# Norms in pairs, dense matmuls while x arrives, and the second weight block ahead of the taps and gate columns

## Chip, cores and metric

The kernel runs on one core of a Trainium2 chip. The metric is the device time of one execution in microseconds (us), the median over several runs. TensorE is called PE, VectorE DVE, ScalarE ACT, GpSimd POOL and SyncE SP.

## What is computed

One inference step of a two-layer decoder for 256 prompt tokens and 8 sample tokens (264 columns in all). The change touches only the first token mixer, a gated DeltaNet with 8 heads of 128:

```python
def gdn_mixer(x, S0, conv_buf, w_in, conv_w, a_log, dt_bias, norm_w, w_out, chunked):
    proj = x @ w_in                                   # 3072 q,k,v channels, 1024 z, 8 a, 8 b
    qkv = proj[..., :GDN_CONV_CH]
    ...
    qkv_c, new_buf = causal_dwconv(qkv, conv_buf, conv_w)   # 4 taps
    qkv_c = jax.nn.silu(qkv_c.astype(f32))
    ...
    q = l2_normalize(q) * (GDN_DK ** -0.5)
    k = l2_normalize(k)
    g = -jnp.exp(a_log.astype(f32)) * jax.nn.softplus(a.astype(f32) + dt_bias.astype(f32))
    beta = jax.nn.sigmoid(b.astype(f32))
    # chunked delta rule: products of k with k and of q with k, decay masks, a triangular inverse ...
    o = o * lax.rsqrt(jnp.mean(jnp.square(o), axis=-1, keepdims=True) + NORM_EPS) * norm_w.astype(f32)
    o = o * jax.nn.silu(z.astype(f32)).reshape(bsz, t, GDN_HEADS, GDN_DV)
    y = o.reshape(bsz, t, GDN_V_W).astype(x.dtype) @ w_out
```

After it come LayerNorm, a dense SwiGLU, a short convolution mixer and a top-2-of-8 expert SwiGLU. They take most of the time and are not changed.

## The kernel before

Every engine runs a program written out by hand, and semaphores alone join them; within an engine, order is program order. So a wait holds everything that stands behind it on that engine.

All weights pass through one ring of **slots** of 1 MB. SP loads slot n into `raw[n % 7]` (`load`). ACT copies it to `high` as fp32r (`split_high`, a 128x2048 activation), DVE forms the rest in `low` (`split_low`, a 128x2048 tensor_tensor), and PE does 32 matmuls with `high` against the two halves of x (`xh`, `xl`), then 16 with `low` (`dense_slot`, lines L392 and L398; L405, L406 and L414 where other matmuls are woven in). `high` has 3 places (`SPLIT`). `split_high` of slot n+3 stands on ACT behind the copies of slot n's result, and `split_low` of slot n+3 stands on DVE behind the convolution of slot n.

**The first mixer** has 16 slots. Slots 0 to 11 give the 24 q, k and v tiles, two per slot. Their results lie in two alternating pairs of PSUM banks, so PE starts slot n only when DVE has convolved slot n-2 (`conv_done`). Slots 12 to 15 give the z tiles, with the sample tokens' decode matmuls (`decode`) woven in. In each round n of the loop ACT does: scaled copies of slot n's result (L722), `split_high` of n+3, Silu of the tiles of slot n-1 (L731). DVE does: the convolution of slot n (six instructions at L1135 and two copies to `utail`), `split_low` of n+3, then whatever belongs to the round.

**Norms.** The q and k tiles form four groups of four tiles (`g` 0 to 3). A group needs Square on ACT (L751), a matmul with ones on PE (`square_sums`), Ln and Exp on ACT (L762, L769), and a multiplication on DVE (`normalise`). `squares` holds one group. PE's sums stand behind slots 3, 5, 7 and 9; ACT's Ln and Exp are in rounds 3, 5, 7 and 9, each behind a load of the activation table that holds both, and the next Silu loads its own table again. `products(k, f)` on PE (8 matmul calls of 128x128 for each k) form k with k and q with k. `decay_exponent`, `decay_masks`, `key_products` and `query_products` are DVE's part of it; then `TT` is made, eight instructions at L1189 and L1192.

**The end of the projections.** Behind slot 15 PE transposes `TT` (L1800). It waits there for `tt0_ready` and for all four increments of `qkm_ready`, which DVE gives in `query_products`:

```python
            for i in range(4):
                c, g = i // 2, i % 2
                pe.wait_ge(tt0_ready, i + 1)
                pe.wait_ge(qkm_ready, 4)
```

POOL makes one multiplication of this stage, `qkv * gB` (L587, 128x1024), once the second q-with-k products are there (`qkp_psum` 2).

**The start.** PE transposes x (8 rounds of k, each of two 128x128 blocks at L1700 and the 8 sample rows at L1701). ACT and DVE make `xh`, `xl` and the residual copy `xres`. SP's queue: x, the sample rows, slot 0, the convolution taps (four transfers), the 16 gate columns `wab`, then slot 1 and on. PE transposes the taps and forms the gate columns behind slot 0.

Of the kernel before, what the change touches and what calls it, by code (L numbers as in the profile page):

```python
# [7 lines left out]
D = 1024  # L8
KT = D // 128
# [53 lines left out]
def hybrid_step(nc, x_prompt, x_sample, state_gdn_S, state_gdn_conv, state_sconv, ln_g, ln_b, gdn_w_in,  # L63
# [8 lines left out]
    with ExitStack() as ctx:  # L72
# [80 lines left out]
        xsnat = place("xsnat", [8, D], at=tt_at)  # L153
# [7 lines left out]
        squares = place("squares", [128, 4, NP], at=t_at + 12 * D)  # L161
# [278 lines left out]

        def turned(s):

            return 4 * s + (0, 0, 4, 8, 8, 8)[s] if s else 0
# [251 lines left out]
        def _(act):  # L695
# [12 lines left out]
            for n in range(1, SPLIT):  # L708
                split_high(act, n)
            act.wait_ge(nat_T, 2)  # L710
            for i in range(2):
                act.activation(taps[:, 12 * i:12 * i + 12, :],
                               bank[4 + i][:, 0:336].rearrange("p (t c) -> p t c", c=28), ACT.Copy).then_inc(taps_ready, 1)
            act.wait_ge(taps_ready, 2)

            for n in range(OUT0):
# [40 lines left out]
                if n in (3, 5, 7, 9):  # L757
                    g = (n - 3) // 2
                    act.preload_act_table_set("natural_log_exp_and_others")
                    for i in range(2):  # L760
                        act.wait_ge(sq_psum, 2 * g + i + 1)
                        act.activation(squares[:, 2 * i:2 * i + 2, :], bank[4 + 2 * (g % 2) + i][:, :]  # L762
                                       .rearrange("p (t i) -> p t i", t=2), ACT.Ln, bias=eps[:, 0:1]).then_inc(sq_log, 1)
# [4 lines left out]
                    act.wait_ge(sq_log, 2 * g + 2)  # L768
                    act.activation(squares[:, :, :], squares[:, :, :], ACT.Exp, scale=-0.5).then_inc(sq_inv, 1)  # L769
                    if n == 5:  # L770
                        act.wait_ge(gcol_ready, 1)
                        act.activation(nbe[:, :, :], gcol[:, :, 0, :], ACT.Exp).then_inc(nbe_ready, 1)
                    if n == 7:
                        for c in range(NCH):
                            act.wait_ge(d_ready, c + 1)
                            act.activation(DM[:, c, :, :], DM[:, c, :, :], ACT.Exp).then_inc(e_ready, 1)
                    if n == 9:
                        act.wait_ge(sq_log, 9)
                        act.activation(ssq[:, :, :], ssq[:, :, :], ACT.Exp, scale=-0.5).then_inc(sq_inv, 1)
                        act.wait_ge(d_ready, 3)  # L780
                        step(act.activation(kd[:, :, :], kd[:, :, :], ACT.Exp))
                        step(act.activation(egl[:, :], gB[:, :, NP - 1], ACT.Exp))
                        step.wait()
                        act.activation(gB[:, :, :], gB[:, :, :], ACT.Exp).then_inc(eg_ready, 1)
                if n == 12:
                    act.wait_ge(gate_in, 64)
                    act.activation(aS[:, :, :], aS[:, :, :], ACT.Exp).then_inc(aS_ready, 1)
                if n == QT // 2:
                    act.wait_ge(sconv_done, 2)
                    act.activation(qkv[:, 16:24, NP:N], qkv[:, 16:24, NP:N], ACT.Silu).then_inc(ssilu_done, 1)  # L790

# [242 lines left out]
        def _(dve):  # L1034
            step = Steps(dve, dve_step)
            for k in range(KT):
                dve.wait_ge(xh_ready, k + 1)
                step(dve.tensor_copy(xres[:, k, :], bank[k][:, 0:N]))
                dve.tensor_tensor(xl[:, k, :], bank[k][:, 0:N], xh[:, k, :].bitcast(F32), ALU.subtract).then_inc(xl_ready, 1)
            for n in range(SPLIT):  # L1040
                split_low(dve, n)
                if n == 0:
# [18 lines left out]
            def normalise(g):  # L1061
# [3 lines left out]
                if g < 2:  # L1065
                    dve.scalar_tensor_tensor(v, v, 128 ** -0.5, squares[:, :, :], ALU.mult, ALU.mult).then_inc(qk_ready, 1)
                else:
                    dve.tensor_tensor(v, v, squares[:, :, :], ALU.mult).then_inc(qk_ready, 1)
# [50 lines left out]
            for n in range(OUT0):  # L1119
# [3 lines left out]
                if n in (4, 6, 8, 10):  # L1123
                    normalise(n // 2 - 2)
# [38 lines left out]
                if n == 8:  # L1163
                    decay_masks(0)
                if n == 9:
                    decay_masks(1)
                if n == 10:
# [6 lines left out]
                    dve.tensor_tensor(kq[:, :, :], q, k, ALU.mult).then_inc(kq_ready, 1)  # L1174
                if n == 11:
                    sample_conv(16, 24)
                    key_products(0)
                if n == 12:
                    dve.wait_ge(mask_ready, 1 + LEVELS)
                    for c in range(NCH):  # L1180
                        step(dve.tensor_tensor(DM[:, c, :, :], DM[:, c, :, :],
                                               upper[:, :].rearrange("p (o i) -> p o i", o=1).to_broadcast([128, 8, CH]), ALU.mult))
                    key_products(1)
                if n == 13:
# [1043 lines left out]
```

## Time and profile before

| | |
|---|---|
| median of 3 runs | 1566.19 us (1565.75 to 1566.3) |
| the profiled execution | 1567.19 us, of which the span is 1565.5 us |
| PE busy | 1531.1 us (98%) |
| DVE busy | 1279.2 us (82%) |
| ACT busy | 1039.8 us (66%) |
| POOL busy | 104.2 us (7%) |

The span is from the first to the last instruction in the trace; all times in rows are counted from its start. Matmul records of one batch overlap, so the pace of PE is read from one start to the next. "L722" is line 722 of the kernel.

### The profile page before, as it was taken

Reading aid. Unit: us, or ns where it says so; the run is one execution under the profiler, and the core shown is the slowest. Engines: PE = TensorE matmul, PEld = TensorE weight load, DVE = VectorE, ACT = ScalarE, POOL = GpSimd, SP = SyncE. Lnnn points to the kernel's source line nnn. Section 1 sums busy time; section 2 is a strip of 40 time slices with the busy share of each in tenths; the row PEclk is TensorE's granted clock in tenths of the full one; section 3 lists DMA queues with packets and bytes.
Section 4 is the critical chain, followed back from the end, with each engine's and each line's share of the span. In section 5 each row is a group of like instructions: output and inputs, shape, how many; then the busy total and the mean of one; then the engine's idle time right before and its main releaser. Section 6 shows DMA issues by size and latency. Waiting matters only on the chain.

```text
span 1565.5 us, 23507 instructions
## 1 busy us (share of the span) xinstructions
PE 1531.1 (98%) x8904; PEld 1342.8 (86%) x8904; DVE 1279.2 (82%) x1285; ACT 1039.8 (66%) x967; POOL 104.2 (7%) x155
## 2 busy tenths in 40 slices
PE   8999999999999999999999999999999999999995
PEld 7899999999999998888888888888888888888883
DVE  6886555787446868999889889889889889889897
ACT  5874335676335447778778778778778778777772
POOL 3106000011000011000000000000000000003100
PEclk9999999999999999999999999999999999999998
DMA  9747605698545539999999999999999999999990
GB/s 290 241 138 275 236 15 188 202 300 283 188 162 190 188 110 373 376 380 383 386 376 374 386 375 373 389 373 378 389 373 371 391 373 377 387 378 373 411 399 28
DMA packets 227447, 476.67 MB, mean 304 GB/s; under 512 B 9692, under 2 KB 69100, under 8 KB 227081
## 3 DMA queue, kind: packets, MB, share of 16 engines
q1 hardware_dynamic: 216040, 435.66, 76.6%
q0 software_dynamic: 11344, 40.12, 7.5%
q8 instruction: 45, 0.74, 0.2%
q14 instruction: 18, 0.15, 0.0%
HBM read 449.74 MB, written 26.24 MB: 304 GB/s over the span
## 4 chain that ended last, share of the span: by engine, by line
PE 89%; DVE 5%; ACT 4%; issue 2%; DMA 0%; DVEq 0%; SPq 0%; ACTq 0%
PE bank L2136 13%; PE bank L2132 12%; PE bank L2133 12%; PE bank L392 12%; PE bank L2161 11%; PE bank L398 6%; PE bank L2167 5%; PE bank L1996 2%; DVE low L357 2%; ACT high L352 2%; PE bank L2144 2%; PE bank L1817 1%; DVE xf L1542 1%; PE bank L2001 1%; PE bank L1833 1%
## 5 line engine op out<-in xcount | busy, mean ns | idle before, releaser
L357 DVE TENSOR_TENSOR low<-raw,high 128x2048 fp32r<-128x2048 f32 x405 | 920.7, 2289 | 147.9 <-ACT high L352 145.3
L352 ACT ACTIVATE high<-raw 128x2048 fp32r<-128x2048 f32 x405 | 775.5, 1918 | 299.1 <-PE bank L2136 92.1
L2132 PE MATMUL bank<-high,xgh 128*128 128x512 f32 x896 | 353.8, 395 | 0.4 <-DVE xgl L1548 0.4
L2133 PE MATMUL bank<-high,xgl 128*128 128x512 f32 x896 | 349.5, 390 | 0.0
L2136 PE MATMUL bank<-low,xgh 128*128 128x512 f32 x896 | 241.3, 391 | 0.9 <-DVE low L357 0.5
L2136 PEld LDWEIGHTS bank<-low,xgh 128*128 128x128 f32 x896 | 167.5, 188 | 39.9 <-DVE low L357 4.6
L2132 PEld LDWEIGHTS bank<-high,xgh 128*128 128x128 f32 x896 | 168.3, 188 | 34.5 <-issue 0.5
L2133 PEld LDWEIGHTS bank<-high,xgl 128*128 128x128 f32 x896 | 168.3, 188 | 33.9
L392 PE MATMUL bank<-xhb,high 128*128 128x266 f32 (+1 forms) x752 | 158.0, 292 | 0.0
L392 PE MATMUL bank<-xlb,high 128*128 128x266 f32 (+1 forms) x752 | 155.0, 287 | 0.0
L2161 PE MATMUL bank<-high,hth 128*128 128x512 f32 x448 | 139.5, 392 | 0.0
L2161 PE MATMUL bank<-high,htl 128*128 128x512 f32 x448 | 138.2, 390 | 0.0
L392 PEld LDWEIGHTS bank<-xhb,high 128*128 128x128 f32 x752 | 119.1, 191 | 2.0 <-issue 1.8
L2167 PE MATMUL bank<-low,hth 128*128 128x512 f32 x448 | 119.9, 389 | 0.0
L392 PEld LDWEIGHTS bank<-xlb,high 128*128 128x128 f32 x752 | 118.9, 191 | 0.0
L398 PE MATMUL bank<-xhb,low 128*128 128x266 f32 (+1 forms) x752 | 100.4, 286 | 0.0
L2161 PEld LDWEIGHTS bank<-high,htl 128*128 128x128 f32 x448 | 84.1, 188 | 17.7
L2167 PEld LDWEIGHTS bank<-low,hth 128*128 128x128 f32 x448 | 84.1, 188 | 17.6
L2161 PEld LDWEIGHTS bank<-high,hth 128*128 128x128 f32 x448 | 82.9, 188 | 16.4
L398 PEld LDWEIGHTS bank<-xhb,low 128*128 128x128 f32 x752 | 95.7, 189 | 0.1
L1009 ACT ACTIVATE sgx<-bank 128x512 f32<-128x512 f32 x56 | 33.6, 600 | 39.4 <-PE bank L2136 39.3
L679 POOL TENSOR_TENSOR flag<-flag 128x1 f32<-128x1 f32 x1 | 3.4, 3352 | 838.2 <-DMA tok<-ysb 838.2
(417 smaller groups left out, 1554.8 us busy)
## 6 DMA issues: line engine op xcount, KB each, us to landing
raw<-in_moe_w_gu_dram SPq DMA_DIRECT2D x224, 1024.0 KB, 6.5
raw<-in_moe_w_down_dram SPq DMA_DIRECT2D x112, 1024.0 KB, 6.6
raw<-in_ffn_w_gu_dram SPq DMA_DIRECT2D x22, 1024.0 KB, 5.1
raw<-in_gdn_w_in_dram SPq DMA_DIRECT2D x16, 1024.0 KB, 8.7
tok<-zeros POOLq DMA_DIRECT2D x26, 512.0 KB, 18.1
raw<-in_sc_w_in_dram SPq DMA_DIRECT2D x12, 1024.0 KB, 5.0
raw<-in_ffn_w_down_dram SPq DMA_DIRECT2D x11, 1024.0 KB, 4.9
s<-in_state_gdn_S_dram POOLq DMA_DIRECT2D x8, 512.0 KB, 6.5
```

The lines of the kernel that those rows point to most:

```text
L352: eng.activation(high[:, n % SPLIT, :], raw[:, n % RAW, :], ACT.Copy).then_inc(high_ready, 1)
L357: eng.tensor_tensor(low[:, n % RAW, :], raw[:, n % RAW, :], high[:, n % SPLIT, :].bitcast(F32), ALU.subtract).then_inc(low_ready, 1)
L392: pe.matmul(out[t], wh[:, k, f[t]], act_[:, k, :], start=k == 0 and act_ is act_h, stop=False)
L398: last = pe.matmul(out[t], wl[:, k, f[t]], act_h[:, k, :], start=False, stop=k == KT - 1)
L1009: act.activation(sgx[:, u % 2, :], bank[2 * (u % 2)][:, :], ACT.Silu).then_inc(sgx_ready, 1)
L1996: pe.matmul(bank[d][:, 0:N], wh[:, k, 128 * d:128 * d + 128], act_[:, f + k, :], start=f + k == 0 and act_ is hh, stop=False)
L2132: pe.matmul(out, xgh[:, 4 * kh + k, :], wh[:, k, :], start=kh + k == 0, stop=False)
L2133: pe.matmul(out, xgl[:, 4 * kh + k, :], wh[:, k, :], start=False, stop=False)
L2136: last = pe.matmul(out, xgh[:, 4 * kh + k, :], wl[:, k, :], start=False, stop=kh == 1 and k == 3)
L2144: last = pe.transpose(bank[6 + u % 2][:, 128 * q:128 * q + 128], hx[:, u % 2, 128 * q:128 * q + 128], idn)
L2161: pe.matmul(bank[4 + g][:, :], src[:, u % 2, hs], wh[:, k, 512 * g:512 * g + 512], start=u + kh + k == 0 and src is hth, stop=False)
L2167: last = pe.matmul(bank[4 + g][:, :], hth[:, u % 2, hs], wl[:, k, 512 * g:512 * g + 512], start=False, stop=u == UNITS - 1 and kh + k == 2)
```

## The change

1. **Pairs.** `squares` holds two groups, at another address (over the later `zgate` and the gates' scratch, so the first Square also waits for `gate_ready`). ACT's Squares are in rounds 2, 4, 7 and 8 (before 2, 4, 6 and 8), and Ln and Exp of two groups at a time in rounds 5 and 9. PE's sums of group 0 stand behind slot 4, of group 1 in the middle of slot 6 (behind its 32 `high` matmuls), of group 2 behind slot 9, of group 3 in the middle of slot 10. DVE's `normalise` calls are in rounds 6, 7, 10 and 11 (before 4, 6, 8 and 10, ahead of the convolution; now behind `split_low`).
2. **Rounds 12 to 15.** The decay exponentials on ACT go from rounds 7 and 9 to round 12, `decay_masks` and `key_products(0)` on DVE to round 12, `key_products(1)` to 13, `TT` and `query_products(0)` from round 13 to 14, `query_products(1)` to 15. PE's four `products` go from behind slots 10 to 13 to behind slots 11 to 14.
3. **Start.** DVE clears a 128-row `xsnat` and sets part of `high`; PE does 11 matmuls of 512 columns on it before x is there, and transposes 128 sample rows in place of 8. The load of the sample rows waits for the clearing, with SP's queue behind it. `split_high` of slot 0 stands behind all eight `xh` copies; six of the eight `xres` copies go from DVE to ACT.
4. **Loads.** Slot 1 is loaded ahead of the taps and `wab`. ACT copies the taps before it splits slot 2.

```diff
@@ sync
             sp_.dma_start(xnat[:, :, :], x_prompt[0].rearrange("(c p) d -> p c d", p=128)).then_inc(x_in, 16)
-            sp_.dma_start(xsnat[:, :], x_sample[:, 0, :]).then_inc(x_in, 16)
+            sp_.wait_ge(acc_ready, 1)
+            sp_.dma_start(xsnat[0:NS, :], x_sample[:, 0, :]).then_inc(x_in, 16)
             for n, src in enumerate(dense):
                 load(sp_, n, src)
-                if n == 0:
+                if n == 1:
@@ scalar
                 act.activation(xh[:, k, :], bank[k][:, 0:N], ACT.Copy).then_inc(xh_ready, 1)
-                if k == 3:
-                    split_high(act, 0)
+            split_high(act, 0)
+            for k in range(2, KT):
+                act.wait_ge(xl_ready, k + 1)
+                act.activation(xres[:, k, :], bank[k][:, 0:N], ACT.Copy).then_inc(acc_ready, 1)
+            split_high(act, 1)
...
-                if n in (2, 4, 6, 8):
-                    g = (n - 2) // 2
+                if n in (2, 4, 7, 8):
+                    g = (2, 4, 7, 8).index(n)
                     act.wait_ge(silu_done, 4 * g + 4)
-                    if g:
-                        act.wait_ge(qk_ready, g)
-                    act.activation(squares[:, :, :], qkv[:, 4 * g:4 * g + 4, 0:NP], ACT.Square).then_inc(sq_ready, 1)
+                    if g == 0:
+                        act.wait_ge(gate_ready, NCH + 1)
+                    if g >= 2:
+                        act.wait_ge(qk_ready, g - 1)
+                    act.activation(group(g), qkv[:, 4 * g:4 * g + 4, 0:NP], ACT.Square).then_inc(sq_ready, 1)
...
-                if n in (3, 5, 7, 9):
-                    g = (n - 3) // 2
+                if n in (5, 9):
+                    pair = (0, 1) if n == 5 else (2, 3)
                     act.preload_act_table_set("natural_log_exp_and_others")
-                    for i in range(2):
-                        act.wait_ge(sq_psum, 2 * g + i + 1)
+                    for g in pair:
+                        for i in range(2):
+                            act.wait_ge(sq_psum, 2 * g + i + 1)
...
+                    for g in pair:
+                        act.wait_ge(sq_log, 2 * g + 2)
+                        act.activation(group(g), group(g), ACT.Exp, scale=-0.5).then_inc(sq_inv, 1)
@@ vector
+            dve.memset(xsnat[:, :], 0.0).then_inc(acc_ready, 1)
+            dve.memset(high[:, SPLIT - 1, 0:640].bitcast(F32), 1.0).then_inc(acc_ready, 1)
             for k in range(KT):
                 dve.wait_ge(xh_ready, k + 1)
-                step(dve.tensor_copy(xres[:, k, :], bank[k][:, 0:N]))
+                if k < 2:
+                    step(dve.tensor_copy(xres[:, k, :], bank[k][:, 0:N]))
...
-                if n in (4, 6, 8, 10):
-                    normalise(n // 2 - 2)
...
+                if n == 6:
+                    normalise(0)
                 if n == 7:
+                    normalise(1)
                     sample_conv(0, 16)
...
-                if n == 13:
+                if n == 14:
                     dve.wait_ge(at_ready, 4)
@@ tensor
+            pe.wait_ge(acc_ready, 2)
+            for i in range(11):
+                pe.matmul(bank[KT - 1][:, :], high[:, SPLIT - 1, 0:128], high[:, SPLIT - 1, 128:640], start=True, stop=True)
             pe.wait_ge(const_ready, 5)
             pe.wait_ge(x_in, 32)
...
                 dense_slot(pe, n, 2 * (n % 2), xh, xl, x_arrives if n == 0 else None,
-                           (lambda t, h: decode(2 * n - 24 + t, h)) if n >= 12 else None)
+                           (lambda t, h: decode(2 * n - 24 + t, h)) if n >= 12 else None,
+                           half=(lambda: square_sums(1 if n == 6 else 3)) if n in (6, 10) else None)
```

How the rows move, at three places. First ACT, round 5, before (L722 copies of slot 5's result, L352 `split_high`, L731 Silu, L762 Ln, L769 Exp):

```order
L722 ACTIVATE qkv<-bank,taps 128x256 x2
L352 ACTIVATE high<-raw 128x2048
L731 ACTIVATE qkv<-qkv 128x256 x2
L759 ACT_TABLE_LOAD
L762 ACTIVATE squares<-bank,eps 128x512 x2
L769 ACTIVATE squares<-squares 128x1024
L772 ACTIVATE nbe<-gcol 128x16
L722 ACTIVATE qkv<-bank,taps 128x256 x2
```

The same round of the change (L730 copies, L739 Silu, L773 Ln, L777 Exp):

```order
L730 ACTIVATE qkv<-bank,taps 128x256 x2
L352 ACTIVATE high<-raw 128x2048
L739 ACTIVATE qkv<-qkv 128x256 x2
L769 ACT_TABLE_LOAD
L773 ACTIVATE squares<-bank,eps 128x512 x4
L777 ACTIVATE squares<-squares 128x1024 x2
L780 ACTIVATE nbe<-gcol 128x16
L730 ACTIVATE qkv<-bank,taps 128x256 x2
```

Two more Ln and one more Exp stand between slot 5's Silu and the copies of slot 6, while round 3 has no Ln and Exp any more.

Second, DVE behind the convolution of slot 6, in the change (L1101 `decay_exponent`, L1079 `normalise`, L1146 and L1149 the convolution of slot 7, then its round):

```order
L357 TENSOR_TENSOR low<-raw,high 128x2048
L1101 TENSOR_SCALAR DM<-gB,gcol 128x128 x8
L1170 TENSOR_TENSOR kd<-gB,gcol 128x16
L1079 SCALAR_TENSOR_TENSOR qkv<-qkv,squares 128x4x256
L1146 SCALAR_TENSOR_TENSOR qkv<-bank,taps,qkv 128x255 x2
L1146 SCALAR_TENSOR_TENSOR qkv<-bank,taps,qkv 128x254 x2
L1146 SCALAR_TENSOR_TENSOR qkv<-bank,taps,qkv 128x253 x2
L1149 COPY utail<-bank 128x11 x2
L357 TENSOR_TENSOR low<-raw,high 128x2048
L1167 SCALAR_TENSOR_TENSOR nbe<-nbe,gcol 128x16
L1079 SCALAR_TENSOR_TENSOR qkv<-qkv,squares 128x4x256
L1089 TENSOR_TENSOR qkv<-taps 128x16x8
```

Before, one `normalise` stood between the convolutions of slots 6 and 8 (group 2, ahead of that of slot 8), and groups 0 and 1 were done ahead of the convolutions of slots 4 and 6. Now groups 0 and 1 are both between those of slots 6 and 8.

Third, the last `split_low` instructions on DVE, before (L1101 `key_products(1)`, L1107 `query_products`):

```order
L1101 TENSOR_TENSOR AT<-bank,AT 128x512 x2
L357 TENSOR_TENSOR low<-raw,high 128x2048
L1189 TENSOR_TENSOR TT<-AT,level_mask 128x512
L1192 TENSOR_TENSOR TT<-ident,TT 128x512
...
L1192 TENSOR_TENSOR TT<-ident,TT 128x512
L1107 TENSOR_TENSOR DM<-bank,DM 128x512 x2
L357 TENSOR_TENSOR low<-raw,high 128x2048
L1107 TENSOR_TENSOR DM<-bank,DM 128x512 x2
```

and in the change (L1114 `key_products(1)`, L1205 and L1208 `TT`, L1120 `query_products`):

```order
L357 TENSOR_TENSOR low<-raw,high 128x2048
L1114 TENSOR_TENSOR AT<-bank,AT 128x512 x2
L357 TENSOR_TENSOR low<-raw,high 128x2048
L1205 TENSOR_TENSOR TT<-AT,level_mask 128x512
L1208 TENSOR_TENSOR TT<-ident,TT 128x512
...
L1208 TENSOR_TENSOR TT<-ident,TT 128x512
L1120 TENSOR_TENSOR DM<-bank,DM 128x512 x4
```

The eight `TT` instructions stood between the `split_low` of slots 16 and 17; now they stand behind that of slot 17, and all of `query_products` behind them.

## Rows read from the trace of the kernel before

**Rows 1.** The page's part 4: the chain that ended last, by engine.

```profile
PE 89%; DVE 5%; ACT 4%; issue 2%; DMA 0%; DVEq 0%; SPq 0%; ACTq 0%
```

**Rows 2.** Timeline of PE, start: start, duration, engine, line, instruction, count [idle before, releaser].

```profile
6.66 0.66 PE L1700 MATMUL bank<-ident,xnat 128*128 128x128 f32 x2 [6.66 <-DMA xsnat<-in_x_sample_dram]
13.19 0.81 PE L392 MATMUL bank<-xhb,high 128*128 128x264 f32 x2
...
31.07 0.41 PE L392 MATMUL bank<-xhb,high 128*128 128x264 f32 x2
```

**Rows 3.** Timeline of ACT and DVE, start.

```profile
23.35 1.92 ACT L352 ACTIVATE high<-raw 128x2048 fp32r<-128x2048 f32 x1 [1.69 <-DMA raw<-in_gdn_w_in_dram]
27.51 2.68 DVE L1135 SCALAR_TENSOR_TENSOR qkv<-bank,taps,qkv 128x255 f32<-128x255 f32 x6
...
30.38 2.28 DVE L357 TENSOR_TENSOR low<-raw,high 128x2048 fp32r<-128x2048 f32 x1
```

**Rows 4.** Timeline of PE, slots 3 to 6.

```profile
40.88 2.11 PE L398 MATMUL bank<-xhb,low 128*128 128x264 f32 x16
...
45.77 2.58 PE L1713 MATMUL bank<-squares,ones 128*128 128x512 f32 x4 [1.95 <-ACT squares L751]
...
53.07 2.11 PE L398 MATMUL bank<-xhb,low 128*128 128x264 f32 x16
...
61.41 1.98 PE L1713 MATMUL bank<-squares,ones 128*128 128x512 f32 x4 [0.35 <-DVE gcol L1149]
...
67.17 2.11 PE L398 MATMUL bank<-xhb,low 128*128 128x264 f32 x16
```

**Rows 5.** Busy time by stretch (PE, PEld, DVE, ACT, POOL), PEclk, DMA share, GB/s.

```profile
48.00:49.00 1.00, 1.00 (x5) 0.85 (x4) 0.96 (x3) 0.98 (x4) 1.00 (x3) 0.50 1.02 393
```

**Rows 6.** Timeline of ACT, round 3.

```profile
45.62 0.82 ACT L722 ACTIVATE qkv<-bank,taps 128x256 f32<-128x256 f32 x2
...
48.14 0.72 ACT L731 ACTIVATE qkv<-qkv 128x256 f32<-128x256 f32 x2
48.88 1.28 ACT L759 ACT_TABLE_LOAD   x1
50.17 1.27 ACT L762 ACTIVATE squares<-bank,eps 128x512 f32<-128x512 f32 x2
51.47 1.06 ACT L769 ACTIVATE squares<-squares 128x1024 f32<-128x1024 f32 x1
```

**Rows 7.** Timeline of DVE, rounds 6 to 8.

```profile
75.26 1.65 DVE L1088 TENSOR_SCALAR DM<-gB,gcol 128x128 f32<-128x128 f32 x8
...
82.08 0.28 DVE L1076 TENSOR_TENSOR qkv<-taps 128x128 f32<-128x128 f32 x1
...
84.25 1.22 DVE L1068 TENSOR_TENSOR qkv<-qkv,squares 128x1024 f32<-128x1024 f32 x1
```

**Rows 8.** Timeline of PE: the last products before slot 12, and slot 12.

```profile
105.30 1.95 PE L1729 MATMUL bank<-qkv 128*128 128x128 f32 x16
107.00 0.37 PE L405 MATMUL bank<-xhb,high 128*128 128x264 f32 x1
```

**Rows 9.** Timeline of DVE, POOL, ACT and PE, slots 14 and 15.

```profile
134.73 3.52 DVE L1192 TENSOR_TENSOR TT<-ident,TT 128x512 f32<-128x512 f32 x1
135.29 2.40 POOL L587 TENSOR_TENSOR qkv<-qkv,gB 128x1024 f32<-128x1024 f32 x1
...
138.17 0.68 DVE L1189 TENSOR_TENSOR TT<-AT,level_mask 128x512 f32<-128x512 f32 x1
...
139.22 0.67 ACT L724 ACTIVATE zgate<-bank 128x264 f32<-128x264 f32 x2 [8.78 <-PE bank L414]
139.78 1.92 ACT L352 ACTIVATE high<-raw 128x2048 fp32r<-128x2048 f32 x1
...
140.83 1.28 DVE L1107 TENSOR_TENSOR DM<-bank,DM 128x512 f32<-128x512 f32 x2
...
148.70 1.91 PE L1800 MATMUL bank<-ident,TT 128*128 128x128 f32 x16
```

More of the change, by code:

```diff
@@ L152, in hybrid_step @@
         xnat = place("xnat", [128, 2, D], at=g_at)
-        xsnat = place("xsnat", [8, D], at=tt_at)
+        xsnat = place("xsnat", [128, D], at=tt_at)
         taps_nat = place("taps_nat", [28, QKV], at=tt_at + 4 * D)
@@ L160, in hybrid_step @@
         s0 = place("s0", [128, 3, HEADS, 128], at=t_at)
-        squares = place("squares", [128, 4, NP], at=t_at + 12 * D)
+        squares = place("squares", [128, 8, NP], at=region + 4 * QT * N)
         bB = place("bB", [128, HEADS, NP], at=tt_at)
@@ L439, in order, with group @@
             return 4 * (s - 1) + 2 * c + g + 1
+        def group(g):
+            return squares[:, 4 * (g % 2):4 * (g % 2) + 4, :]
         def turned(s):
@@ L713, in _ @@
                                bank[4 + i][:, 0:336].rearrange("p (t c) -> p t c", c=28), ACT.Copy).then_inc(taps_ready, 1)
+            for n in range(2, SPLIT):
+                split_high(act, n)
             act.wait_ge(taps_ready, 2)
@@ L756, in _ @@
                     act.activation(ssq[:, :, :], qkv[:, 0:16, NP:N], ACT.Square).then_inc(sq_ready, 1)
-                if n in (3, 5, 7, 9):
-                    g = (n - 3) // 2
+                if n in (5, 9):
+                    pair = (0, 1) if n == 5 else (2, 3)
                     act.preload_act_table_set("natural_log_exp_and_others")
-                    for i in range(2):
-                        act.wait_ge(sq_psum, 2 * g + i + 1)
-                        act.activation(squares[:, 2 * i:2 * i + 2, :], bank[4 + 2 * (g % 2) + i][:, :]
-                                       .rearrange("p (t i) -> p t i", t=2), ACT.Ln, bias=eps[:, 0:1]).then_inc(sq_log, 1)
+                    for g in pair:
+                        for i in range(2):
+                            act.wait_ge(sq_psum, 2 * g + i + 1)
+                            act.activation(group(g)[:, 2 * i:2 * i + 2, :], bank[4 + 2 * (g % 2) + i][:, :]
+                                           .rearrange("p (t i) -> p t i", t=2), ACT.Ln, bias=eps[:, 0:1]).then_inc(sq_log, 1)
+                    for g in pair:
+                        act.wait_ge(sq_log, 2 * g + 2)
+                        act.activation(group(g), group(g), ACT.Exp, scale=-0.5).then_inc(sq_inv, 1)
+                    if n == 5:
+                        act.wait_ge(gcol_ready, 1)
+                        act.activation(nbe[:, :, :], gcol[:, :, 0, :], ACT.Exp).then_inc(nbe_ready, 1)
                     if n == 9:
@@ L790, in _ @@
                     act.activation(qkv[:, 16:24, NP:N], qkv[:, 16:24, NP:N], ACT.Silu).then_inc(ssilu_done, 1)
+                    act.preload_act_table_set("natural_log_exp_and_others")
+                    for c in range(NCH):
+                        act.wait_ge(d_ready, c + 1)
+                        act.activation(DM[:, c, :, :], DM[:, c, :, :], ACT.Exp).then_inc(e_ready, 1)
+                    act.wait_ge(d_ready, 3)
+                    step(act.activation(kd[:, :, :], kd[:, :, :], ACT.Exp))
+                    step(act.activation(egl[:, :], gB[:, :, NP - 1], ACT.Exp))
+                    step.wait()
+                    act.activation(gB[:, :, :], gB[:, :, :], ACT.Exp).then_inc(eg_ready, 1)
+                    act.wait_ge(gate_in, 64)
+                    act.activation(aS[:, :, :], aS[:, :, :], ACT.Exp).then_inc(aS_ready, 1)
             for i in range(4):
@@ L1174, in _ @@
                     dve.tensor_tensor(kq[:, :, :], q, k, ALU.mult).then_inc(kq_ready, 1)
+                if n == 10:
+                    normalise(2)
                 if n == 11:
+                    normalise(3)
                     sample_conv(16, 24)
+                if n == 12:
+                    for c in range(NCH):
+                        decay_masks(c)
                     key_products(0)
-                if n == 12:
                     dve.wait_ge(mask_ready, 1 + LEVELS)
@@ L1709, in square_sums @@
                 pe.wait_ge(sq_ready, g + 1)
+                if g == 1:
+                    pe.wait_ge(gcol_ready, 1)
+                    pe.wait_ge(taps_ready, 3)
                 if g >= 2:
@@ L1712, in square_sums @@
                 for i in range(2):
[L1713 removed]
+                    pe.matmul(bank[4 + 2 * (g % 2) + i][:, :], ones[:, :], group(g)[:, 2 * i:2 * i + 2, :].rearrange("p t i -> p (t i)"),
                               start=True, stop=True).then_inc(sq_psum, 1)
```

54 lines of the change are left out of this document (14 added, 40 removed).

## The prediction

> **What bounds the kernel now.** I read the page's chain first: PE holds 89% of it [rows 1]. So the question is where PE stands still or runs slowly, and the change touches only the first 150 us. There the timeline of PE, read from start to start, shows the losses. From 31.07 to 40.88 lie one slot and the `high` part of the next, 80 matmuls in 9.81 us [rows 2, 4]: 0.1226 us each, so a slot is 5.88 us (3.93 with `high`, 1.95 with `low`). The first loss is at slot 3: its `low` part begins at 40.88 and ends at 42.83, the small transposes take 1.0 us, then PE waits 1.95 us for the first Square, until 45.77 [rows 4]. After this wait the granted clock is at half, 1.2 GHz, in 48 to 49 us [rows 5]. From the sums to the next `low` part it takes 7.30 us (45.77 to 53.07) here, 5.76 us at slot 6 (61.41 to 67.17) [rows 4]: the clock costs 1.54 us beside the wait. The sums cost 5.76 - 3.93 = 1.83 us each. From slot 12 on PE runs through: 107.00 to 148.70 [rows 8, 9] are four slots and two sets of products (1.70 us each, 105.30 to 107.00 [rows 8]), so such a slot takes 9.57 us.
>
> **The change, part by part.** I carry PE, ACT and DVE forward from these rows.
>
> *Start.* The 11 matmuls, the cleared rows and the reordered copies change when slot 0 runs, but not when slot 2 may: slot 2 needs the convolution of slot 0, which stands on DVE behind `split_low` of slot 2, and that behind the landing of slot 2's weights at 23.35 [rows 3]. SP sends the same bytes ahead of slot 2 in either order, so I leave that landing where it is. The convolution ends at 30.38 [rows 3], and slot 2 started at 31.07 [rows 2]; it can now start at 30.5. Gain 0.6 us. The cover is the slack of slots 0 and 1. If the 11 matmuls run past 6.66, when x was there [rows 2], or leave the clock low, the eight rounds of transposes, 6.53 us before (6.66 to 13.19 [rows 2]) and wider now, end later, `split_high` of slot 0 behind them too, and up to 2 us of loss reach slot 2. In the other direction nothing ahead of 30.4 is to be won.
>
> *Slots 2 to 6.* Slot 2 at 30.5, slot 3 to 42.3, small transposes to 43.3, and no wait for a Square: slot 4 to 49.2, sums to 51.0, slot 5 to 56.9, slot 6 with sums in its middle to 64.7. Before it ended at 67.17 + 1.95 = 69.1 [rows 4]. The lead is 4.4 us: the wait of 1.95, the clock's 1.54, 0.6 from the start, the rest from a 0.35 us wait [rows 4].
>
> *Where the lead goes.* ACT's round 5 begins at 57.2: copies 0.7, `split_high` 1.8, Silu 0.75, table 1.3, then four Ln (two take 1.3) and two Exp (1.0 each) [rows 6]. It ends at 66.5, while slot 6's result is there at 64.9. DVE gets it at 67.3 and from then on is late: convolution and `utail` 2.9 (27.51 to 30.38 [rows 3]), `split_low` 2.2, `decay_exponent` with its tail 1.65, `normalise` 1.15 (it takes 1.22 [rows 7] with some overlap), convolution 2.9: slot 7 is convolved at 78.05. PE ended slot 8 at 76.5, so slot 9 waits 1.6 us. DVE goes on with `split_low` 2.2, `normalise` 1.2, the sample convolution 2.2 (82.08 to 84.25 [rows 7]), convolution 2.9: 86.5. PE, after slot 9 (84.0) and sums (85.5), waits 1.1 us for slot 10. Sums of group 3 stand in its middle, at 90.6; their Ln follows at 91.5, and ACT comes out of its pair and the sample norms at 95.4. Slot 10's copies end at 96.2, its convolution at 99.1, `split_low` at 101.3, the sample products at 102.0 and `normalise` of group 2 at 103.2. PE has slot 11 done at 100.5 and waits 2.8 us for that with `products`. Slot 12 starts at 105.0, and one set of products (1.7) is still owed against the 107.0 of before [rows 8]: of 4.4 us of lead, 0.2 is left. Four table loads of 1.28 us [rows 6] are saved on ACT, but ACT waits for PE's sums where they would count.
>
> *Slots 12 to 15.* Slot 14 ends at 105.0 + 3 x 9.57 + 2 x 1.70 = 137.2, then PE has products and slot 15: 11.3 us, to 148.5. DVE has to do behind slot 14: ACT's copies 0.76, `split_high` 1.9 (139.22 to 139.78 and on [rows 9]), `split_low` 2.2, eight `TT` instructions (four take 138.17 to 140.83, 2.66 us, so 5.3 [rows 9]) and two `query_products` of 1.2 (1.28 [rows 9]): 12.7 us with hand-overs, to 149.9. PE's transposes at L1800 wait for all of it. Before, they began at 148.70 with no wait [rows 9].
>
> POOL adds to it. Its multiplication takes 2.40 us, and the DVE instruction that met it took 3.52 us, where its likes take 0.68 [rows 9]: 2.8 us of delay. Now it is released by the products behind slot 14, at 139.2, just ahead of DVE's last `split_low` (139.9), which reads two SBUF tiles as the held instruction did. The bounds are 0 and 2.8 us; I take 1.75, the time to POOL's end at 141.6, since the POOL instruction starts first. The transposes begin at 151.65, 2.95 us later than before. (The Trainium skill, SBUF — State Buffer, "Who interferes with whom", says that a DVE instruction with two SBUF inputs and a GpSimd one that reads SBUF exclude each other, and that whichever issues first keeps the ports for the whole instruction. By that rule the delay would be the same 1.75. In the rows the DVE instruction starts at 134.73, ahead of POOL's 135.29, and is yet the one held: the trace agrees on the exclusion, not on the order.)
>
> *Clock.* The wait of 1.95 us brought the clock to half and cost 1.54 us [rows 4, 5]. The waits of 2.8 us (ahead of slot 12) and 3.1 us (ahead of L1800) are longer. The first costs 0 to 1.54, I take 1.54, and all behind it moves along. The second falls on small dependent matmuls, so part is hidden: 0 to 1.54, I take 1.2. That of slot 9 is hidden, since DVE is late there anyway.
>
> Behind the mixer nothing changes, and PE is bound there, so the difference stays: 2.95 + 1.54 + 1.2 = **+5.7 us**. The profiled execution would go from 1567.19 to 1572.9; the median of the runs is 1.0 lower, 1566.19, so I say **1571.9**. About 0.2% (3.1 us) is what a measurement of this kernel tells from no change.
>
> **Rivals.**
> 1. *As above, new waits on DVE.* 1569.3 to 1576. Chance 0.60, with the clock costs from 0.2 to 3.1 us, and 2 us more should the start also be late (0.1 of the 0.60).
> 2. *The same order, but the clock stays up and POOL does not hold DVE.* 1.2 to 3.0 us: 1567.4 to 1569.2. For it: the waits are sums of many steps, and one of 1 us less would be too short. Against it: [rows 4, 5]. Within 0.2%, chance 0.27 with all small outcomes, also that of a change which moves nothing.
> 3. *The lead survives* (the other side). The place is DVE between slots 6 and 10. If its queue were some 5 us shorter there than I count, PE would not wait at slots 9 and 10 nor for `products`, and slot 12 would start at 99.8 by PE's own work (64.7, five slots, two sums, 0.3 for the sample norms and 1.7). Slot 14 then ends at 131.9 and DVE, with POOL's hold, 14.4 us behind it at 146.4: 2.3 us faster, 1563.9; with POOL's hold at its lower bound 4.1 us faster, 1562.1; and 5.5 us, 1560.7, only if the end on DVE were free too. Of the 5.5 us of middle waits nearly all must go before it passes 0.2%. Against it: DVE's steps are priced by rows. Chance of over 0.2% faster 0.13.
>
> **Range.** 1564.5 to 1576.0: below it lies most of rival 3, above it a late start together with all clock costs. The likeliest case alone is 1569.3 to 1575.
>
> **What would show it.** Right: no wait behind slot 3; slot 6 ends near 64.7; slot 9 waits for a convolution; a wait of some 2.8 us before the first `products`; the last `split_low` before `TT` near 4 us long; L1800 waits about 3 us for DVE and starts near 153 on the trace's clock. Wrong: slot 2 starts well off 30.5 (weights land at another time), DVE's rows between 67 and 103 have idle time, or the clock stays at 2.4 GHz through the waits.

## The result and the profile after

The change makes the kernel slower: 1574.06 us median of 5 runs (1572.96 to 1576.39) against 1566.19 (1565.72 to 1566.38), ratio 1.0048, 95% interval 1.0036 to 1.0060. That is +7.9 us; the forecast was +5.7. The profiled execution of the changed kernel is the fastest of its five, 1572.96 us, with a span of 1571.2 us against 1565.5: +5.7 us in the spans.

The timeline of PE after the change (start, duration, engine, line, instruction, count, [idle before, releaser]), in the same stretches as [rows 2, 4, 8, 9]:

```profile
2.74 4.57 PE L1706 MATMUL bank<-high 128*128 128x512 f32 x11 [2.74 <-DVE high L1047]
...
12.21 0.52 PE L392 MATMUL bank<-xhb,high 128*128 128x264 f32 x2 [2.28 <-ACT high L352]
...
40.05 2.11 PE L398 MATMUL bank<-xhb,low 128*128 128x264 f32 x16
...
48.96 1.88 PE L1735 MATMUL bank<-squares,ones 128*128 128x512 f32 x4
...
60.47 1.88 PE L1735 MATMUL bank<-squares,ones 128*128 128x512 f32 x4
61.79 2.52 PE L398 MATMUL bank<-xhb,low 128*128 128x264 f32 x16
...
68.07 2.11 PE L398 MATMUL bank<-xhb,low 128*128 128x264 f32 x16
...
77.38 0.51 PE L392 MATMUL bank<-xhb,high 128*128 128x264 f32 x2 [1.32 <-DVE utail L1149]
...
85.83 0.51 PE L392 MATMUL bank<-xhb,high 128*128 128x264 f32 x2 [0.59 <-DVE utail L1149]
...
102.69 3.42 PE L1751 MATMUL bank<-qkv 128*128 128x128 f32 x16 [2.90 <-DVE qkv L1081]
105.86 0.37 PE L405 MATMUL bank<-xhb,high 128*128 128x264 f32 x1
...
152.37 2.71 PE L1821 MATMUL bank<-ident,TT 128*128 128x128 f32 x16 [2.85 <-DVE DM L1120]
154.88 4.64 PE L1838 MATMUL bank<-T,AT 128*128 128x128 f32 x32
159.36 3.69 PE L1854 MATMUL bank<-P,TT 128*128 128x64 f32 x32
162.88 1.37 PE L1865 MATMUL bank<-ident,T 128*128 128x128 f32 x11
```

The wait for the first Square is gone, and the sums of group 1 stand in the middle of slot 6, whose `low` part starts at 61.79 where it started at 67.17 before [rows 4]: 5.4 us earlier. Then four new waits follow, all for DVE: 1.32, 0.59, 2.90 and 2.85 us. Slot 12 starts at 105.86, 1.1 us ahead of the 107.00 of [rows 8], but with one set of products still to come. The transposes of `TT` start at 152.37, 3.67 us behind the 148.70 of [rows 9].

DVE and POOL at slots 14 and 15 after the change, by their timelines:

```profile
140.60 3.92 DVE L357 TENSOR_TENSOR low<-raw,high 128x2048 fp32r<-128x2048 f32 x1 [7.75 <-ACT high L352]
144.44 0.68 DVE L1205 TENSOR_TENSOR TT<-AT,level_mask 128x512 f32<-128x512 f32 x1
...
149.75 2.48 DVE L1120 TENSOR_TENSOR DM<-bank,DM 128x512 f32<-128x512 f32 x4
```

```profile
140.00 2.37 POOL L592 TENSOR_TENSOR qkv<-qkv,gB 128x1024 f32<-128x1024 f32 x1 [5.84 <-PE bank L1751]
```

DVE stands idle for 7.75 us ahead of `split_low`, then `split_low`, `TT` and all of `query_products` lie in one chain that PE waits for. `split_low` takes 3.92 us beside POOL's row, where it takes 2.29 alone.

The clock, by windows of the trace (a row gives the length of the window, the busy times of PE, PEld, DVE, ACT and POOL with their counts, and then, third from its end, the granted clock as a share of 2.4 GHz):

```profile
102.00:106.00 4.00, 3.31 (x17) 3.31 (x18) 3.89 (x10) 1.08 (x3) 0.00 (x0) 0.57 0.58 203
...
154.00:156.00 2.00, 2.00 (x12) 2.00 (x11) 0.04 (x1) 1.60 (x4) 2.00 (x7) 0.50 1.02 371
```

Behind both long waits the clock is at or near 1.2 GHz. From the transposes of `TT` to the next transposes (L1865) it takes 10.51 us (152.37 to 162.88). Before it took 8.85, from the 148.70 of [rows 9] to this row of the kernel before:

```profile
157.55 1.91 PE L1844 MATMUL bank<-ident,T 128*128 128x128 f32 x16
```

So the clock costs 1.66 us there (the run with POOL moved, below, takes 8.87 with the clock up), and at 162.88 the changed kernel is 5.33 us behind.

### The profile page after: what moved, and what is told of

It is laid out like the page before. It is cut to its first block, busy times and chain, and to the rows that moved or that the text cites. A ratio compares the mean times of both kernels' runs of the same rounds, so it can differ in the third digit from the quotient of the medians.

```text
span 1571.2 us, 23528 instructions
## 1 busy us (share of the span) xinstructions
PE 1533.6 (98%) x8915; PEld 1347.0 (86%) x8915; DVE 1276.6 (81%) x1281; ACT 1035.9 (66%) x969; POOL 104.0 (7%) x155
## 4 chain that ended last, share of the span: by engine, by line
PE 87%; DVE 7%; ACT 3%; issue 2%; DVEq 0%; ACTq 0%
PE bank L2157 13%; PE bank L2153 12%; PE bank L2154 12%; PE bank L392 11%; PE bank L2182 10%; PE bank L398 6%; PE bank L2188 5%; PE bank L2017 2%; DVE low L357 2%; ACT high L352 2%; PE bank L2165 2%; PE bank L1838 1%; DVE xf L1558 1%; PE bank L2022 1%; PE bank L1854 1%
## 5 line engine op out<-in xcount | busy, mean ns | idle before, releaser
L352 ACT ACTIVATE high<-raw 128x2048 fp32r<-128x2048 f32 x405 | 775.4, 1918 | 292.3 <-PE bank L2157 91.4
```

The costliest lines, as they stand in the source:

```text
L352: eng.activation(high[:, n % SPLIT, :], raw[:, n % RAW, :], ACT.Copy).then_inc(high_ready, 1)
```

## The experiments

They ran in three groups, each on one chip together with the kernel before; differences are from its median in the same group (1566.83, 1566.68 and 1567.28 us). My theory: DVE's queue sets the four new waits, and the clock adds to the two long ones. Its rivals: the start costs it; or the pairs are harmless and the tail alone counts.

**The start and the loads alone.** The kernel before with parts 3 and 4 of the change (the cleared rows, the dense matmuls, the order of loads and copies).

```diff
+            pe.wait_ge(acc_ready, 2)
+            for i in range(11):
+                pe.matmul(bank[KT - 1][:, :], high[:, SPLIT - 1, 0:128], high[:, SPLIT - 1, 128:640], start=True, stop=True)
...
-                if n == 0:
+                if n == 1:
```

> The kernel before with the start and the loads of the change alone (parts 3 and 4); norms, products and the rounds stay as before. Theory (the pairs cost the time, the start is hidden behind the convolution of slot 0): slot 2 starts near 30.2 in place of 31.07 and everything behind it moves along, 0.9 us faster, 1565.3. Rival (the start costs, by 11 matmuls, wider transposes and a low clock in slot 0): 1 to 3 us slower, 1567 to 1569.

Measured 1564.37 us (1563.62 to 1568.94), ratio 0.9986 (0.9977 to 0.9995): 2.5 us faster. The start is not what costs. It gains more than the 0.6 us of the prediction and the 0.9 us expected here, and the timeline of PE shows where:

```profile
45.13 1.98 PE L1723 MATMUL bank<-squares,ones 128*128 128x512 f32 x4 [1.45 <-ACT squares L755]
50.89 2.11 PE L398 MATMUL bank<-xhb,low 128*128 128x264 f32 x16
```

Slot 2 starts only 0.3 us earlier (30.77), but ACT's Square comes 0.64 us earlier (45.13 against 45.77), PE waits 1.45 in place of 1.95 us, and is at the next `low` part 5.76 us later, not 7.30 as in [rows 4]: the clock stayed at 2.4 GHz. In this execution the 1.54 us of the clock are saved together with half a microsecond of wait.

**The pairs alone.** The changed kernel with the start and the loads of before.

```diff
-            pe.wait_ge(acc_ready, 2)
-            for i in range(11):
-                pe.matmul(bank[KT - 1][:, :], high[:, SPLIT - 1, 0:128], high[:, SPLIT - 1, 128:640], start=True, stop=True)
...
-                if n == 1:
+                if n == 0:
```

> The changed kernel with the start and the loads of the kernel before: the pairs of norms and the moved rounds alone (parts 1 and 2). Theory: all of the loss, and the 0.9 us of the start missing, so 1 us above the changed kernel, 1574 to 1576, with the waits ahead of the first products and ahead of the transposes of TT, each near 2.9 us. Rival (the start costs): at most 2 us above the kernel before, 1568.

Measured 1574.64 us (1570.84 to 1578.04), ratio 1.0045 (1.0031 to 1.0059): 7.8 us slower, the whole loss. The waits are the same to 0.01 us (1.32, 0.60, 2.90 and 2.85), each 1.7 us later than in the changed kernel, because slot 2 starts 1.7 us later (31.92 against 30.20):

```profile
31.92 0.40 PE L392 MATMUL bank<-xhb,high 128*128 128x264 f32 x2
...
104.41 3.41 PE L1741 MATMUL bank<-qkv 128*128 128x128 f32 x16 [2.90 <-DVE qkv L1074]
...
154.07 2.71 PE L1810 MATMUL bank<-ident,TT 128*128 128x128 f32 x16 [2.85 <-DVE DM L1113]
```

The 1.7 us are those of two executions. By the medians the start is worth only 0.1 us with the pairs (7.8 us slower without it, 7.9 with it), and the medians of such kernels are not sure to a microsecond: the executions of this one lie 7.2 us apart.

**`TT` ahead of the last `split_low`.** In the changed kernel the eight `TT` instructions and `query_products(0)` go ahead of `split_low` of slot 17; all else is as in the change.

```diff
+                if n == 14:
+                    dve.wait_ge(at_ready, 4)
...
+                    query_products(0)
+                    split_low(dve, n + SPLIT)
-                if n == 14:
-                    dve.wait_ge(at_ready, 4)
```

> The changed kernel with the eight TT instructions and the first query products ahead of the last split on DVE (slot 17) in round 14, as the order was before. Theory: TT begins near 133 in place of 144.4, PE no longer waits ahead of the transposes of TT, and the clock stays up there: 2.85 + 1.67 = 4.5 us less than the changed kernel, 1569 to 1570. Rival (PE's wait there is not DVE's order but the clock and the late slots before it): under 1 us.

Measured 1568.52 us (1565.80 to 1570.45), ratio 1.0009 (1.0000 to 1.0017): 1.7 us slower than before, 6.2 less than the change, where 4.5 were expected. DVE's 7.75 us of idle time takes the work, and the transposes start at 147.86 without a wait. The wait of 2.90 us for the products is still there, but in this profile the clock did not fall behind it:

```profile
102.56 2.05 PE L1752 MATMUL bank<-qkv 128*128 128x128 f32 x16 [2.90 <-DVE qkv L1081]
104.37 0.37 PE L405 MATMUL bank<-xhb,high 128*128 128x264 f32 x1
...
147.86 1.91 PE L1822 MATMUL bank<-ident,TT 128*128 128x128 f32 x16
```

```profile
102.00:106.00 4.00, 3.44 (x30) 3.44 (x31) 3.90 (x10) 0.95 (x3) 0.00 (x0) 1.00 0.55 193
```

The products take 1.81 us to slot 12, against 3.17 in the changed kernel (102.69 to 105.86), after the same wait. This profiled execution took 1566.24 us, 2.3 less than the median of its kernel.

**POOL's multiplication later.** In the changed kernel POOL also waits for all four `query_products`, so that it no longer meets `split_low`.

```diff
             pool.wait_ge(qkp_psum, 2)
+            pool.wait_ge(qkm_ready, 4)
```

> The changed kernel with POOL's multiplication held back until the query products are done, so that it cannot meet DVE's last split. Theory (POOL holds DVE for 1.6 us there): that split takes 2.29 us in place of 3.92, the transposes of TT start 1.6 us earlier with a wait of 1.2 us, and such a short wait leaves the clock up more often: 1.6 to 3.3 us less than the changed kernel. Rival (the wait has another cause): no difference.

Measured 1570.18 us (1568.68 to 1571.93), ratio 1.0022 (1.0013 to 1.0031): 3.5 us slower than before, 4.4 less than the change, where 1.6 to 3.3 were expected. `split_low` and the transposes of `TT`:

```profile
140.09 2.29 DVE L357 TENSOR_TENSOR low<-raw,high 128x2048 fp32r<-128x2048 f32 x1 [7.75 <-ACT high L352]
```

```profile
150.23 1.94 PE L1822 MATMUL bank<-ident,TT 128*128 128x128 f32 x16 [1.23 <-DVE DM L1121]
...
159.10 1.91 PE L1866 MATMUL bank<-ident,T 128*128 128x128 f32 x16
```

`split_low` is 1.63 us shorter and the wait 1.62 us shorter: POOL's hold falls on the path whole. Behind the shorter wait the clock stayed up, and the way to the next transposes is 8.87 us (150.23 to 159.10), not 10.51. So in these two executions 1.6 us of hold bring 1.6 us of clock with them, 3.3 us in all. The rest of the 4.4 is not POOL's by anything that is shown: this profile is 0.7 us ahead at the products already (101.96), because its clock stayed up in slot 0 and slot 2 started at 29.38. The transposes start 2.14 us earlier (152.37 to 150.23), and with 1.64 us of the tail that is 3.8 of the 4.3 us between the spans; 0.5 us I can't place.

**`normalise(2)` ahead of the convolution of slot 10.** In the changed kernel the third `normalise` moves ahead, all else as in the change.

```diff
+                if n == 10:
+                    normalise(2)
...
-                if n == 10:
-                    normalise(2)
```

> The changed kernel with the normalisation of group 2 on DVE ahead of the convolution of slot 10, where DVE stood idle for 2.66 us, in place of behind it. Theory (the wait of 2.90 us ahead of the first products is DVE's order and nothing else): that wait goes, and the 1.4 us of clock behind it: 2.9 to 4.3 us less than the changed kernel, the wait ahead of the transposes of TT stays at 2.85. Rival (the lead is lost on ACT or PE itself, by the longer pairs): under 1 us.

Measured 1569.35 us (1566.43 to 1570.87), ratio 1.0014 (1.0005 to 1.0022): 2.7 us slower than before, 5.2 less than the change, where 2.9 to 4.3 were expected. The products start at 100.34 with no wait and slot 12 2 us later at full clock. The tail is as in the change:

```profile
100.34 1.95 PE L1751 MATMUL bank<-qkv 128*128 128x128 f32 x16
...
148.83 3.43 PE L1821 MATMUL bank<-ident,TT 128*128 128x128 f32 x16 [2.85 <-DVE DM L1120]
```

The clock fell behind the last wait here too. That wait is 2.85 us again, since DVE's chain there hangs on PE's slot 14 and moves with it.

**The sums of group 0 in the middle of slot 4, in the kernel before.** Nothing of the pairs; only the wait of 1.95 us is attacked.

```diff
+                           half=(lambda: square_sums(0)) if n == 4 else None)
...
-                if n in (3, 5, 7, 9):
+                if n in (5, 7, 9):
```

> The kernel before with one edit: the sums of squares of group 0 stand in the middle of slot 4 in place of ahead of it. Theory (the wait of 1.95 us and the 1.54 us of clock behind it are real losses, and the pairs were not needed to win them): 3 to 3.5 us faster, 1562.7 to 1563.2. Rival (ACT or DVE is the bound there and PE's wait is slack): within 1 us of the kernel before.

Measured 1565.52 us (1564.62 to 1567.72), ratio 0.9992 (0.9984 to 1.0001): 1.3 us faster by the medians, with no change inside the interval, so the expectation of 1562.7 to 1563.2 failed. The timeline of PE shows why:

```profile
32.12 0.40 PE L392 MATMUL bank<-xhb,high 128*128 128x264 f32 x2
...
50.26 2.52 PE L398 MATMUL bank<-xhb,low 128*128 128x264 f32 x16
...
60.07 1.98 PE L1713 MATMUL bank<-squares,ones 128*128 128x512 f32 x4 [1.42 <-DVE gcol L1149]
```

The wait and the clock's loss are gone and slot 4's `low` part starts at 50.26, 2.8 us ahead of the 53.07 of [rows 4], although slot 2 started 1.05 us later in this execution (32.12 against 31.07). But the next sums wait 1.42 us for DVE's copy of the gate columns (the bank that they write), which stands in DVE's round 4. I had not asked what the sums of group 1 wait for once PE is early.

**That copy earlier, with the start.** The kernel before with the start and the loads, the sums of group 0 in the middle of slot 4, and the copy of the gate columns in DVE's round 3.

```diff
-                if n == 4:
+                if n == 3:
                     dve.wait_ge(gcol_psum, 1)
```

> The kernel before with the start and loads of the change, the sums of group 0 in the middle of slot 4, and DVE's copy of the gate columns in round 3 in place of round 4 (PE waited 1.42 us for it when the sums alone were moved). No pairs. Theory: 0.9 us of the start, 3.5 us of wait and clock at slot 4, less what DVE and ACT give back behind it: 1561.5 to 1563.5. Rival (ACT's single norms bound the stage): 1564.5 as the start alone.

Measured 1563.77 us (1562.19 to 1564.75), ratio 0.9977 (0.9968 to 0.9987): 2.9 us faster than before, 0.3 us short of the range expected. The wait for the copy is gone; waits of 0.84 and 0.82 us for Squares take its place (at 57.32 and 85.59).

**Three moves on DVE together.** The changed kernel, with `TT` and `query_products(0)` ahead of the last `split_low`, `normalise(2)` ahead of the convolution of slot 10, and both `decay_exponent` calls and their tail from rounds 5 and 6 to round 11.

```diff
-                if n == 5:
...
-                    decay_exponent(0)
-                if n == 6:
-                    decay_exponent(1)
...
                     normalise(3)
                     sample_conv(16, 24)
+                    decay_exponent(0)
+                    decay_exponent(1)
```

> The changed kernel with three orders on DVE mended: TT ahead of the last split, the normalisation of group 2 ahead of the convolution of slot 10, and the decay exponents of rounds 5 and 6 (1.65 us each) in round 11, where DVE is idle. Theory: no wait of PE over 1 us between slot 3 and the end of the stage, so the lead of 5.3 us of slot 6 is kept: 1560 to 1562. Rival (the pairs themselves cost more than they save): not under 1565.

Measured 1562.29 us (1562.06 to 1562.90), ratio 0.9969 (0.9958 to 0.9981): 4.4 us faster than before, so 12.3 less than the change, and 0.3 us short of the range expected. Of the waits in the middle one of 0.52 us is left, and the products and the transposes of `TT` have none:

```profile
85.03 0.51 PE L392 MATMUL bank<-xhb,high 128*128 128x264 f32 x2 [0.52 <-DVE utail L1151]
...
98.83 1.95 PE L1750 MATMUL bank<-qkv 128*128 128x128 f32 x16
...
144.32 1.91 PE L1820 MATMUL bank<-ident,TT 128*128 128x128 f32 x16
```

POOL still holds `split_low` here, 3.91 us at 135.56; nothing waits for it.

**The same without the dense matmuls.**

```diff
-            for i in range(11):
-                pe.matmul(bank[KT - 1][:, :], high[:, SPLIT - 1, 0:128], high[:, SPLIT - 1, 128:640], start=True, stop=True)
```

> The kernel with the three moves on DVE (TT first, normalise ahead, decay exponents late), without the 11 dense matmuls at the start; all else equal. Theory: nothing ahead of the convolution of slot 0 decides when slot 2 starts, so the dense matmuls only set the pace of the x transposes and of slot 0, which lie under the wait of slot 2 (1.44 us there). x transposes take longer again (0.8 us for each round of k in place of 0.33), slot 0 starts up to 2 us later, slot 2 near 31.0 to 31.5; time 1562.3 to 1563.0. Rival: the start matters as a whole, slots 0 and 1 run at the low clock, ACT's and DVE's rows follow, and slot 2 comes 1.5 us or more later: 1564 or more.

Measured 1563.44 us (1562.93 to 1565.18), ratio 0.9975 (0.9965 to 0.9984): 3.8 us faster than before where the kernel with them was 4.4, and 0.4 us above the range expected. The intervals overlap, and the spans of the two profiles are 1561.3 and 1561.2. But all ten executions without them (1562.93 to 1565.18 us) took longer than the six with them (1562.06 to 1562.90, in the other group, where the kernel before was 0.6 us faster) and than the five of the next run, with them and in the same group (1561.40 to 1562.86). PE's timeline without them, the first transposes, a later round, slot 0 and slot 2, and DVE's last copy of the convolution of slot 0:

```profile
6.53 0.66 PE L1716 MATMUL bank<-ident,xnat 128*128 128x128 f32 x2 [6.53 <-DMA xsnat<-in_x_sample_dram]
...
10.33 0.38 PE L1716 MATMUL bank<-ident,xnat 128*128 128x128 f32 x2
...
13.10 0.81 PE L392 MATMUL bank<-xhb,high 128*128 128x264 f32 x2 [2.28 <-ACT high L352]
...
31.05 0.41 PE L392 MATMUL bank<-xhb,high 128*128 128x264 f32 x2
```

```profile
30.31 0.24 DVE L1151 COPY utail<-bank 128x11 f32<-128x11 f32 x2
```

Slot 2 with them:

```profile
31.01 0.51 PE L392 MATMUL bank<-xhb,high 128*128 128x264 f32 x2 [1.44 <-DVE utail L1151]
```

Without them the transposes start slowly (0.66 us for the first round of k, 0.33 at the end), slot 0 starts at 13.10 (12.92 with them) at the low clock, and slot 2 at 31.05 (31.01 with them). The two starts of slot 2 are alike for different reasons. With the dense matmuls PE is early and waits 1.44 us for the convolution of slot 0, which is late because the weights of slot 2 came late (ACT splits them at 23.84). Without them they came earlier (23.44), the convolution is done at 30.55, and PE comes straight from slot 1, half a microsecond later. So they are not covered whole, against what the prediction said: in this execution their absence costs 0.5 us (30.55 to 31.05), and in one like that of the changed kernel, where ACT splits these weights at 22.92 and slot 2 starts at 30.20 without a wait, it would be 0.85 us (an estimate from the two starts, 31.05 and 30.20). The medians give 0.6 us (4.4 and 3.8), within their intervals.

**The same with POOL's multiplication later.** All three moves on DVE and the wait on `qkm_ready` for POOL.

```diff
             pool.wait_ge(qkp_psum, 2)
+            pool.wait_ge(qkm_ready, 4)
```

> The kernel with the three moves on DVE, and POOL's multiplication released only by all four query_products (as in the run that moved POOL alone). Theory: with TT and query_products ahead of the last split_low, the transposes of TT have slack, so the 1.6 us by which POOL holds split_low (3.9 us in place of 2.3) are worth nothing: 1562.3, within 0.1%. split_low is back at 2.3 us. POOL's row comes earlier than in the run that moved it alone (query_products are earlier) and may hold another instruction. Rival: split_low of slot 17 feeds slot 17, behind the mixer, and its delay is passed on: 1560.7, 1.6 us faster.

Measured 1561.77 us (1561.40 to 1562.86), ratio 0.9963 (0.9949 to 0.9976). `split_low` is back at 2.29 us, and the time is the same within the intervals as with the hold (0.9969), as expected. The same 1.6 us, worth some 3.3 us in the changed kernel (wait and clock), is worth nothing that can be told where DVE has slack. This is the fastest kernel of the study, 5.5 us under the one before.

## Why the prediction was right, and where its sizes were off

Its forecast, slower by new waits on DVE, came true: 1574.06 us lies in the range and 2.2 us above the 1571.9. By its steps:

- **Start.** Slot 2 at 30.5: it started at 30.20, without a wait. The size came out near, but the reading behind it was wrong. The prediction took the convolution of slot 0 for what sets slot 2, so that only 0.6 us was to be won. In the kernel before PE came to slot 2 at 31.07 straight from slot 1, some 0.6 us behind that convolution: PE itself was last. It was so in all three traces with the old start (31.07, 31.92 and 32.12). In the eight with the new one slot 2 starts at 29.38 to 31.01, and whether PE or the convolution is last depends on when slot 2's weights land (ACT splits them at 22.04 to 23.84); the prediction held that at 23.35. That the forecast 0.6 us met 0.87 in this trace is luck. Alone the start gave 2.5 us, and in its trace the clock also stayed up at slot 3, behind a shorter wait.
- **The lead.** Slot 6 was to end at 64.7; slot 7's `low` part started at 68.07, and its `high` part is 3.93 us, so slot 6 ended at 64.1.
- **Waits of slots 9 and 10.** 1.6 and 1.1 us forecast, 1.32 and 0.59 measured; and 2.8 us before the products, 2.90 measured. I had carried DVE's queue some 0.6 us too late here: the products started at 102.69, forecast 103.3. A slip is in the sum as well: the sums of group 2 go in at 1.5 us (84.0 to 85.5) where the prediction's own price is 1.83, so slot 10 should have waited 0.8 us and not 1.1. Moving DVE work out of this stretch, and `normalise(2)` into its idle time, left 0.52 us of these 4.8, so the cause is shown.
- **Slots 12 to 15.** A hold of 1.75 us by POOL was forecast, 1.63 measured, and shown by moving POOL away. The transposes were to start at 153.2 on the trace (151.65 with the 1.54 of the clock); they did at 152.37, after 2.85 us (forecast 3.1).
- **Clock.** 1.54 and 1.2 us forecast. The products took 1.36 us longer to slot 12 than in the run where the clock stayed up; the tail cost 1.66 us, not 1.2. The small dependent matmuls hid nothing of it here.
- **The sum.** At 162.88 us the kernel is 5.33 us behind, forecast 5.69; with 0.4 us more that come up behind the mixer, the spans differ by 5.7. That they agree so well is in part luck: 0.8 us too much in the middle and 0.5 too little at the tail.
- **The step that was furthest off** is the last one, from profile to median: "the median of the runs is 1.0 lower". The profiled execution of the changed kernel is 1.1 us below its median, so 2.1 of the 2.2 us missed lie in this step. The five executions of the changed kernel spread over 3.4 us, the five of before that it is compared with over 0.7; over the 29 and 28 executions of the first two groups, though, the kernel before spreads over 4.7 and 5.2 us. Likely it is the clock, which falls behind a long wait in some executions and not in others. The mean granted clock of every execution is on record and bears this out in part. Of the twelve with `normalise(2)` ahead, the six at 0.992 and 0.993 took 1569.52 to 1570.87 us, the six at 0.994 and 0.995 1566.43 to 1569.17; of the pairs alone, the one at 0.996 took 1570.84 and the one at 0.991 1578.04. In the changed kernel the slowest has the lowest (0.990), but the other four, at 0.992 and 0.993, don't come in that order. Only one execution of each kernel has a trace, so where in the kernel the clock fell in the others is not shown.

Rival 3, the lead that survives, needed some 5 us less on DVE between slots 6 and 10. The three moves on DVE made nearly that kernel, with the end on DVE free too, for which the rival gave 5.5 us of gain: 4.4 were measured. Rival 2, a clock that stays up and POOL that doesn't hold DVE, gave a loss of 1.2 to 3.0 us. The run with POOL moved is close to it, with 3.5 us; in its trace the clock was still low behind the wait for the products. The upper end of the range, 1576.0, was wider than the prediction's own terms: 1.05 us more of POOL's hold, all clock costs and a late start add up to 1575.3.

## What to carry to other kernels

A wait that is taken away from PE is a gain only as far as the next engine is ahead; carry that engine's queue forward, row by row, before moving work behind it, and ask of each later wait what releases it once PE is early (the copy of the gate columns was missed so). Work that several engines wait for (`TT`, `normalise(2)`) belongs in the idle time ahead of a large split, not behind it. And a wait on PE is worth its own length plus what the clock loses behind it: here 1.4 to 1.7 us, in some executions. Last, where two engines arrive at nearly the same time, as PE and DVE at slot 2, one trace doesn't tell which of them sets the start: compare several.

## What the runs showed of the hardware that I had not expected

- The clock behind a wait on PE is not settled by the wait's length alone. In the first 170 us of the twelve traces it fell to 1.2 GHz behind six of the seven waits of 2.85 to 2.91 us (it stayed up in the run with `TT` first), behind six of the nine of 2.28 us ahead of slot 0, and behind the one of 1.95 us [rows 5]; behind the ten of 1.1 to 1.45 us it never did. Where it fell on work that PE was bound by, it cost 1.4 to 1.7 us. Ahead of slot 0 it fell in the changed kernel, in spite of the dense matmuls, and stayed up in the one with the three moves. (The Trainium skill, TensorE: Matmul & The Clock Gate, "Part 1: The HAM clock gate", says that the chip watches PE's activity on a schedule of its own, which does not begin anew with the kernel, so that the point of a change depends on where the work lands in it. That would fit both this and the spread of the runs; no run here tests it.) The window of the changed kernel at slot 0:

```profile
14.00:15.00 1.00, 1.00 (x7) 1.00 (x6) 0.48 (x1) 1.00 (x1) 1.00 (x2) 0.50 1.13 131
```

- DVE's tensor_tensor and POOL's exclude each other for the whole instruction, and POOL's never grew: 2.40, 2.37, 2.37 and 2.39 us in four kernels, met or not, while DVE's went from 2.29 to 3.92 and 3.91. With POOL 0.6 us ahead, DVE's row lasted until POOL's end (142.37) and its own 2.29 us more, less 0.14. In [rows 9], where DVE's row began 0.56 us ahead of POOL's, it lasted until POOL's end (137.69) and its own 0.69 us more, less 0.13. (The Trainium skill, SBUF — State Buffer, "Who interferes with whom", says that the one that issues first keeps the ports. This case agrees where POOL was first; in [rows 9] DVE's row began first and was held all the same.)
